# One-block expert groups: VectorE's first bounds and activation placed ahead of the lo parts of the seventh weight half

## What is computed

```python
def expert_block(args):
    xe, e = args                                  # 128 tokens, their expert
    gu = xe @ w_gate_up[e] + b_gate_up[e]         # 1024 -> 2048
    gate, up = jnp.split(gu, 2, axis=-1)
    gate = jnp.minimum(gate, SWIGLU_LIMIT)
    up = jnp.clip(up, -SWIGLU_LIMIT, SWIGLU_LIMIT)
    act = gate * jax.nn.sigmoid(SWIGLU_ALPHA * gate) * (up + 1)
    return act @ w_down[e] + b_down[e]
```

## Time and profile before

| | us |
|---|---|
| median of 3 runs | 2389.17 |
| lowest and highest of the 3 | 2384.26 and 2391.97 |
| the profiled execution, its own time | 2392.84 |
| its span (first to last instruction) | 2391.2 |
| expert stage within the span | 740 to 2391 |

### The profile page before, as it was taken

The page is one execution under the profiler, slowest core; times in us unless marked ns, Lnnn a source line. Parts: engine busy times, 40 slices in busy tenths (PEclk is TensorE's granted clock), DMA queues, the critical chain, the costliest instruction groups (busy, mean ns, idle before and its releaser), DMA issues.

```text
span 2391.2 us, 37523 instructions
## 1 busy us (share of the span) xinstructions
PE 2255.1 (94%) x10570; PEld 1819.6 (76%) x10571; DVE 1742.3 (73%) x2124; ACT 1293.0 (54%) x1736; POOL 794.3 (33%) x784
## 2 busy tenths in 40 slices
PE   6899997888976999999999999999999999999997
PEld 2679876776764788888878888878888887878886
DVE  1684423577765799976689866687999768689697
ACT  2332212675324677755567655566777556576575
POOL 2153003792234233432223222232333322233242
PEclk9899998899987999999999999999999999999999
DMA  7134205882235899987689967697999868799695
GB/s 245 61 128 146 59 17 131 249 224 78 106 115 200 288 370 372 372 290 232 215 283 373 361 216 231 224 321 241 368 378 361 302 215 276 261 330 371 230 352 176
DMA packets 299220, 583.98 MB, mean 244 GB/s; under 512 B 23889, under 2 KB 53601, under 8 KB 297057
## 3 DMA queue, kind: packets, MB, share of 16 engines
q1 hardware_dynamic: 269248, 501.68, 60.2%
q0 software_dynamic: 26560, 69.06, 10.6%
q10 hardware_dynamic: 3362, 12.59, 1.4%
HBM read 544.79 MB, written 44.24 MB: 246 GB/s over the span
## 4 chain that ended last, share of the span: by engine, by line
PE 62%; DVE 4%; issue 2%; DVEq 1%; DMA 0%; ACT 0%; ACTq 0%; POOL 0%; POOLq 0%
PE psum L2036 55%; DVE d_wlo L1863 3%; PE psum L2018 3%; PE psum L1976 2%; PE psum L1986 2%; DVE d_up L1876 0%; DMA d_xg<-xn_d,d_entry 0%; DVE d_act L1882 0%; DMA d_entry<-list_d 0%; DVE d_atlo L1888 0%; DVEq L1542 0%; DVE d_y_two L1853 0%; DVEq L1541 0%; ACT d_y_two L1764 0%; DVEq L1540 0%
## 5 line engine op out<-in xcount | busy, mean ns | idle before, releaser
L1863 DVE TENSOR_TENSOR d_wlo<-d_raw,d_whi 128x1024 fp32r<-128x1024 f32 x578 | 673.8, 1218 | 81.5 <-ACT d_whi L1739 79.9
L1739 ACT ACTIVATE d_whi<-d_raw 128x1024 fp32r<-128x1024 f32 x578 | 574.6, 1053 | 117.8 <-PE psum L2036 86.0
L2036 PE MATMUL psum<-d_whi,d_xthi 128*128 128x512 f32 x1152 | 458.7, 398 | 0.1
L2036 PE MATMUL psum<-d_whi,d_xtlo 128*128 128x512 f32 x1152 | 454.6, 395 | 0.0
L2036 PE MATMUL psum<-d_wlo,d_xthi 128*128 128x512 f32 x1152 | 454.5, 394 | 0.0
L1863 DVE TENSOR_TENSOR d_wlo<-slab,d_whi 128x1024 fp32r<-128x1024 f32 x292 | 343.5, 1218 | 15.4 <-ACT d_whi L1739 13.6
L1642 POOL DMA_INDIRECT out_dram<-d_yst,d_dest x49 | 93.3, 1905 | 781.5 <-DVE d_yst L1910 724.8
L1739 ACT ACTIVATE d_whi<-slab 128x1024 fp32r<-128x1024 f32 x292 | 292.5, 1054 | 6.0 <-PE psum L2036 5.6
L2036 PEld LDWEIGHTS psum<-d_whi,d_xtlo 128*128 128x128 f32 x1152 | 217.0, 188 | 50.7
L2036 PEld LDWEIGHTS psum<-d_whi,d_xthi 128*128 128x128 f32 x1152 | 217.0, 188 | 50.0 <-issue 1.6
L2036 PEld LDWEIGHTS psum<-d_wlo,d_xthi 128*128 128x128 f32 x1152 | 217.2, 189 | 48.3
(11 more groups left out here) (322 smaller groups left out, 3984.4 us busy)
## 6 DMA issues: line engine op xcount, KB each, us to landing
slab<-in_w_gate_up_dram SPq DMA_DIRECT2D x144, 1024.0 KB
d_raw<-in_w_gate_up_dram SPq DMA_DIRECT2D x144, 1024.0 KB, 9.0
d_raw<-in_w_down_dram SPq DMA_DIRECT2D x144, 1024.0 KB, 7.1
b_wp<-in_w_ada_dram POOLq DMA_DIRECT2D x16, 1024.0 KB, 7.7
slab<-in_w_in_dram SPq DMA_DIRECT2D x12, 1024.0 KB, 5.5
slab<-in_w_ada_dram SPq DMA_DIRECT2D x8, 1024.0 KB
a_xin<-in_x_dram ACTq DMA_DIRECT2D x2, 2048.0 KB
v_d<-a_vst POOLq DMA_DIRECT2D x16, 256.0 KB, 2.7
```

Of the source, the lines that this page charges most:

```text
L1739: nc.scalar.activation(whi[n % NW][:, part, :], raw[n % NRAW][:, part, :], ACT.Copy).then_inc(whi_ok, 1)
L1863: nc.vector.tensor_tensor(wlo[n % NW][:, part, :], raw[n % NRAW][:, part, :], whi[n % NW][:, part, :].bitcast(F32), ALU.subtract).then_inc ...
L2036: mm = nc.tensor.matmul(to, m_[:, KH * h + k, :], w_[n % NW][:, k, :], start=(h == 0 and k == 0 and q == 0), stop=(h == 1 and k == KH - 1 ...
```

## The change

Only the condition under which VectorE runs its bounds and activation is edited. For two-block groups nothing changes (n = 4 and 8, and n // 8 is 0 and 1 as n // 4 - 1 was). For one-block groups the first pair moves from iteration 4 to iteration 3; the second stays in iteration 8.

```diff
-                        if n in (4, 8):
+                        if n in ((4, 8) if blocks == 2 else (3, 8)):
                             for b in range(blocks):
-                                clipped(g, n // 4 - 1, b, sh)
+                                clipped(g, n // 8, b, sh)
                             for b in range(blocks):
-                                activated(g, n // 4 - 1, b, sh)
+                                activated(g, n // 8, b, sh)
```

## The result

| | before | after |
|---|---|---|
| median of 11 runs (us) | 2391.32 | 2396.05 |
| lowest and highest | 2384.26 and 2392.34 | 2392.79 and 2400.74 |
| span of the profiled execution | 2391.2 | 2395.1 |

The ratio of after to before is 1.0025, with a 95% interval of 1.0018 to 1.0033: the changed kernel is slower by 6.0 us (4.3 to 7.9). The difference of the medians is 4.7 us.

What follows compares the result with a forecast made beforehand. TensorE was taken to set the pace, with VectorE and transfers close behind. Terms 0 (seven first groups) + 5.1 (17 following groups) + 0 (queues) on the 2389.17 us median gave 2394.3 us, range 2386 to 2402.

Steps and rivals of the forecast that it cites:

- The seven first groups: One-block groups first after a two-block group: second activation still ends at 836.20, the 0.7 us wait stays, term 0.
- The 17 following groups: One-block groups behind one-block groups: bounds wait for half 3, second turn 0.30 us late in each, 5.1 us in all.
- the wake: Time from the start of half 3's last matmul to VectorE's bounds, taken as 0.43 us from another stage.
- slack of 0.11: At TensorE's second turn in following groups, 0.11 us of the second activation's 0.41 us delay was spare.
- The upper bound of 0.41: Following groups: lo 9 and 10 0.03 longer and wake 0.08 longer would give 0.41 x 17 = 7.0 us.
- The rule weighed against the rows: Moved bounds and activation: free semaphore by the skill page gives 2.0 us; the trace's 0.78 us spacing gives 5.1.
- Queues at nothing: SyncE's loads issue up to 3.28 us later, 2.8 us of slack remain at ScalarE, GpSimd unaffected; costed at nothing.
- The other signs: Trace after: VectorE idle 1.9 us (0.6 to 0.9 in 13), 24 second-turn waits, about 10 us total, repeat 36.9 us.
- the larger stall at the same place: Following groups: waits at first bounds and activation add up, 0.41 to 0.5 each, 7.7 us, time 2396.9; chance 0.09.
- the rival in which the move costs nothing: Second turn: larger slack or earlier half 3 signal, so nothing reaches TensorE; time 2389.2; chance 0.18.
- The late loads: Transfers in one-block groups: later issue not made up, at most 1.1 us per group, 18 us, time 2407; chance 0.08.
- The faster case: First groups: the seven second-turn waits vanish, 4.9 us, time 2384.3, needing a 0.7 us VectorE hole; chance 0.07.

Runs made afterwards that it cites:

- e_wait: Kernel before, order kept, with one wait added on VectorE ahead of lo 6 for half 3's last matmul in one-block groups; ratio 1.0029, 6.9 us slower.
- e_between: Kernel before, with the first bounds and activation placed between the two instructions of lo 6 in one-block groups; ratio 0.9993.
- e_second: Kernel before, with the second bounds and activation moved to iteration 7 and the second d_atlo to iteration 8 in one-block groups; ratio 1.0025.
- e_gap: e_second plus one VectorE wait ahead of lo 4 for half 1 in one-block groups; ratio 0.9977 to the kernel before, median 2385.77 against 2391.04.
- e_wake: Changed kernel, with the semaphore raised by 1 at the bias and 1 at the closing matmul, not 2 at closing; ratio 1.0033 to the kernel before.
- e_both: e_second with the first pair also moved to iteration 3, as in the changed kernel; ratio 1.0008 to the kernel before.

## Why the prediction was right

*What bounds it.* Right: TensorE sets the pace, and only its waits moved the time.

*The seven first groups, 0.* Right: VectorE's work up to the second activation is the same sum, and the wait stayed at 0.70.

*The 17 following groups, 17 x 0.30 = 5.1 us.* The mechanism was right, by e_wait (the wait alone costs the same) and e_between (a wait within the slack costs nothing). The size was low by a quarter: 6.85 us in the trace, 0.40 a group, 0.42 in the group shown. The term that was mis-sized is the wake. I took 0.43 us from another stage; here it is 0.51 (928.68 to 929.19), in all 17. The stage that I took it from has both values. In the same trace of the kernel before, the same two instructions stand 0.51 apart 11 us later:

```profile
284.44 0.39 PE L609 MATMUL psum<-a_hlo,a_whi 128*128 128x512 f32 x1
284.95 0.69 DVE L544 TENSOR_TENSOR a_ucv<-psum,convn 128x512 f32<-128x512 f32 x1 [1.27 <-PE psum L609]
```

Of the eight times that L609 woke L544 there, six are at 0.43 and two at 0.50 to 0.51; I read one. The steps behind the wake came out as counted, within 0.01: 1.41, 3 x 2.27, 0.60, 4.54 and 1.48 us. From the start of half 3's last matmul to the second activation's end it was 15.35 us (928.68 to 944.03) where I had 15.26. That lifts 0.30 to 0.39, and 0.39 is what TensorE shows over this stretch: from half 3's last matmul to the one behind the second turn it took 15.82 us (928.68 to 944.50), before 15.43 (930.99 to 946.42). So the slack of 0.11 was right too. The last 0.03 of the 0.42 lies between the second turn and the next half 3 (907.50 to 928.68 is 21.18, 909.84 to 930.99 was 21.15); its cause is open. The upper bound of 0.41 in the prediction held a longer wake and two slower lo parts; of the two, the runs showed the wake alone.

*The rule weighed against the rows.* The Trainium skill, VectorE: DVE Perf Modes, section on the DRAIN you can't avoid, has a semaphore between two Vector instructions cost nothing extra. At the new place the dependent pair is again 0.80 us apart (929.19 to 929.99) and the next instruction 0.61; the sum by the rule, 2.0 us, lies outside the interval of 4.3 to 7.9, that by the row inside it. The row decides.

*Queues at nothing.* Right in what it cost. One sign that I had named for being wrong, that ScalarE waits for loads, did appear, 1.0 and 0.3 us; but it lies ahead of the first one-block group, so it says nothing of the move.

*The other signs.* The 24 waits, VectorE's idle time ahead of the first bounds (1.86 us in four groups, 0.87 to 0.94 in 13) and the lost gaps came as said, and the repeat is 37.0 where I had 36.9. TensorE's total of waits was to be about 10 us and reads 7.8, since the view puts each of the 17 at 0.17.

*The rivals.* The nearest was the larger stall at the same place, 0.41 to 0.5 a group, priced at 7.7 us for 0.45. The measured 0.40 lies nearer to it than to my 0.30, and the interval of 4.3 to 7.9 us holds both sums, so the time alone does not tell them apart. The traces do: the gaps and the 0.11 of slack took up their part of the wait, as in the forecast, and only the wake was longer. The interval excludes the rival in which the move costs nothing. The late loads did not come. The faster case needed a hole in VectorE's row of work in the first groups; there was none. That those seven waits could be removed was shown by e_second and e_gap, through the second pair.

*The numbers.* 2394.3 was forecast as 5.1 us above the median of before; measured are 2396.05 and 1.0025, inside the range and within 0.3%. How near 5.1 comes is in part luck. The medians differ by 4.7 us, the ratio says 6.0, the traces 6.85, and the same kernel again 8.4.

What stays open: why VectorE wakes 0.51 us after a matmul's start in all 17 groups here, and after 0.43 or 0.51 in the first stage. It is not the raise by 2 (e_wake), and not the reading of PSUM, since in e_wait the instruction that wakes, at 930.96, reads none and is no faster.

## What to carry to other kernels

Before you move an instruction forward on an engine that serves the bounding one, ask when its input is ready. A wait put ahead of independent work gives up the time that this work covered. It costs what is left after all the slack on the way to the next thing that the bounding engine needs. Count both from start to start, since recorded lengths overlap by some 0.1 us and the gaps alone (0.58 and 0.67) come out too small. Here the wait adds 1.96 us (924.96 + 2.27 to 929.19). The slack along the queue was 1.46: 0.66 ahead of the first `d_atlo` (2.93 behind the start of lo 8, below, less 2.27), 0.77 ahead of lo 9 (1.37 less 0.60) and 0.03 in lo 9 and 10. At the end of it 0.11 was spare. That leaves 0.39.

```profile
935.50 2.35 DVE L1863 TENSOR_TENSOR d_wlo<-d_raw,d_whi 128x1024 fp32r<-128x1024 f32 x2
```

Where an engine is late at one point, bring forward what is needed there, not what comes first: the second activation was the late one, and moving the first could not help it.

An engine off the critical path may live on another's pauses. Filling VectorE without a gap took away GpSimd's time to issue its scatter, and the loss came back 20 us later as a missing gather.

## What the runs showed of the hardware

An indirect DMA instruction of GpSimd can be held up for as long as VectorE's `d_wlo` instructions, which read two SBUF operands each, follow one another without a pause. The scatter (L1642) takes 1.6 to 1.7 us in groups where VectorE is idle. Beside back-to-back `d_wlo` instructions it ends 1.52 us behind the last of them, whatever follows:

| kernel | last `d_wlo` ends | behind it on VectorE | scatter ends | its length |
|---|---|---|---|---|
| e_gap | 923.80 | pause of 0.10 us | 925.32 | 3.04 |
| before | 926.19 | pause of 1.08 us | 927.71 | 5.31 |
| e_both | 925.16 | pause of 1.33 us | 926.68 | 7.58 |
| e_second | 930.82 | the first bounds, no pause | 932.34 | 9.86 |

In the nine traces 50 scatters of this stage took 3 us or more, and all 50 ended 1.50 to 1.54 us behind such a row's end. So the length of the pause does not matter, 0.10 us is enough, and an instruction that reads PSUM (the bounds) does as well as a pause. The row alone does not hold the scatter, though. In 13 groups of e_second it took 2.3 to 2.4 us and ended 1.9 to 6.4 us before the row did; there VectorE had paused 0.2 us between the end of `d_yst`, which releases GpSimd, and the scatter's start:

```profile
961.31 4.63 DVE L1863 TENSOR_TENSOR d_wlo<-d_raw,d_whi 128x1024 fp32r<-128x1024 f32 x4 [0.22 <-issue]
961.68 2.38 POOL L1642 DMA_INDIRECT out_dram<-d_yst,d_dest  x1 [10.57 <-DVE d_yst L1910]
```

The Trainium skill, SBUF — State Buffer, section "SBUF: two separate sides", says that VectorE and GpSimd share a pair of ports under an exclusive lock, and that a VectorE instruction with two SBUF inputs holds it against a GpSimd one that reads SBUF. The four lengths agree with it in kind. By the page the lock is held for one instruction; here GpSimd did not get through between instructions that followed without a pause, and did in 0.10 us. That the lock is the cause is argued from these lengths. The bounds of e_second, which read no SBUF operand, are the nearest thing to a test of it; a VectorE instruction of one SBUF input in the place of a `d_wlo` was not tried.
